# Router logits in four column groups, token rows dealt out anew, and a branch turned round, in a two-layer mixture-of-experts step

## The reference, cut to what matters

```
def moe_swiglu(h, w_router, w_gu, w_down):
    t = h.reshape(B * L, D)
    logits = (t @ w_router).astype(jnp.float32)
    top_v, top_i = lax.top_k(logits, TOP_K)
    top_w = jax.nn.softmax(top_v, axis=-1)
    gates = jnp.einsum('nk,nke->ne', top_w, one_hot(top_i, N_EXPERTS))
    gu = jnp.einsum('nd,edf->enf', t, w_gu)
    g, u = jnp.split(gu, 2, axis=-1)
    eo = jnp.einsum('enf,efd->end', jax.nn.silu(g) * u, w_down)
    y = jnp.einsum('ne,end->nd', gates, eo)

h = rms_norm(x, g_ffn) * (1 + scale2) + shift2
x = x + gate2 * moe_swiglu(h, ...)
```

## Time and profile before

| what | value |
|---|---|
| median of 3 runs | 1887.8 us (1887.16 to 1888.7) |
| the profiled execution | 1886.11 us |
| its span, from the first to the last instruction | 1884.3 us |
| PE busy | 97% of the span |
| DVE / ACT / POOL busy | 59% / 42% / 7% |
| moved by DMA | 290.56 MB, a mean of 154 GB/s |

### The profile page before, as it was taken

One profiled execution on the slowest core, in us unless ns is written; L12 is line 12 of the kernel. 1 busy time (PEld: TensorE's weight loads), 2 busy tenths in 40 slices (PEclk: granted clock), 3 DMA queues, 4 the chain that ended last, 5 costly groups with the idle time before them and its releaser, 6 DMA issues.

```text
span 1884.3 us, 30889 instructions
## 1 busy us (share of the span) xinstructions
PE 1818.4 (97%) x12347; PEld 1680.9 (89%) x12347; DVE 1115.4 (59%) x1907; ACT 789.5 (42%) x1335; POOL 141.1 (7%) x109
## 2 busy tenths in 40 slices
PE   7999989999999999999999889799999999999988
PEld 6999857999999999999999569698989989899886
DVE  2643786544432343456536874476778778778777
ACT  4222264422211222233221554165656656666565
POOL 2000000200000000020000001222000000002221
PEclk8999999999999999999999999899999999999999
DMA  9435100422423224233254001196787778778862
GB/s 363 161 116 217 64 1 1 135 101 101 146 79 112 101 101 146 79 113 123 79 191 145 12 1 23 75 234 215 255 255 248 266 226 277 263 238 292 314 221 79
DMA packets 93847, 290.56 MB, mean 154 GB/s; under 512 B 15368, under 2 KB 23944, under 8 KB 93696
## 3 DMA queue, kind: packets, MB, share of 16 engines
q1 hardware_dynamic: 86784, 271.20, 43.2%
q0 software_dynamic: 6912, 17.30, 2.7%
HBM read 281.98 MB, written 12.28 MB: 156 GB/s over the span
## 4 chain that ended last, share of the span: by engine, by line
PE 87%; DVE 6%; issue 2%; DMA 2%; ACT 2%; POOL 1%; SPq 0%; POOLq 0%; ACTq 0%; DVEq 0%
PE ps L776 48%; PE ps L1144 11%; PE ps L1167 5%; PE ps L1145 5%; PE ps L1177 4%; PE ps L842 3%; PE ps L971 2%; PE ps L917 2%; PE ps L1155 2%; PE ps L1148 2%; DVE nbias L2099 1%; PE ps L1147 1%; DVE pr L2116 1%; DVE w_lo L1943 1%; DMA yab<-y_rows,late 1%
## 5 line engine op out<-in xcount | busy, mean ns | idle before, releaser
L1943 DVE TENSOR_TENSOR w_lo<-raw,w_hi 128x1024 fp32r<-128x1024 f32 x394 | 482.3, 1225 | 345.8 <-ACT w_hi L1383 337.8
L1383 ACT ACTIVATE w_hi<-raw 128x1024 fp32r<-128x1024 f32 x394 | 414.5, 1054 | 315.7 <-PE ps L776 170.8
L1144 PE MATMUL ps<-hg,w_hi 128*128 128x320 f32 (+5 forms) x1232 | 346.8, 351 | 5.0 <-DVE w_lo L1943 3.7
L776 PE MATMUL ps<-a_hi,w_hi 128*128 128x320 f32 x1472 | 341.4, 313 | 3.4 <-DVE a_lo L1974 3.4
L776 PE MATMUL ps<-a_hi,w_lo 128*128 128x320 f32 x1472 | 336.5, 310 | 0.0
L776 PE MATMUL ps<-a_lo,w_hi 128*128 128x320 f32 x1472 | 333.5, 307 | 0.0
L1145 PE MATMUL ps<-hg,w_lo 128*128 128x160 f32 (+5 forms) x1232 | 301.0, 244 | 0.0
L776 PEld LDWEIGHTS ps<-a_hi,w_hi 128*128 128x128 f32 x1472 | 247.0, 188 | 12.1 <-issue 8.1
L776 PEld LDWEIGHTS ps<-a_lo,w_hi 128*128 128x128 f32 x1472 | 248.5, 188 | 0.0
L776 PEld LDWEIGHTS ps<-a_hi,w_lo 128*128 128x128 f32 x1472 | 245.0, 188 | 0.0
L1144 PEld LDWEIGHTS ps<-hg,w_hi 128*128 128x128 f32 x1232 | 232.9, 189 | 6.6 <-DVE w_lo L1943 4.2
(11 more groups left out here) (321 smaller groups left out, 2599.3 us busy)
## 6 DMA issues: line engine op xcount, KB each, us to landing
raw<-gu_w SPq DMA_DIRECT2D x220, 512.0 KB, 4.7
raw<-moe_down_w SPq DMA_DIRECT2D x88, 512.0 KB, 4.4
ada_raw<-ada_w SPq DMA_DIRECT2D x21, 2048.0 KB, 8.2
raw<-in_w SPq DMA_DIRECT2D x48, 512.0 KB, 9.7
raw<-down_w SPq DMA_DIRECT2D x22, 512.0 KB, 3.4
raw<-out_w SPq DMA_DIRECT2D x16, 512.0 KB, 3.6
ada_pro<-ada_w SPq DMA_DIRECT2D x2, 2048.0 KB, 18.8
y_rows<-ey POOLq DMA_DIRECT2D x7, 512.0 KB
```

Source lines behind the costliest of these rows:

```text
L776: ins = nc.tensor.matmul(out[:, hf, 0:c1 - c0], w, o[:, c0:c1], start=f, stop=e)
L1144: nc.tensor.matmul(sums, whi, both, start=(k == 0), stop=False)
L1383: nc.scalar.activation(w_hi[:, s, :], raw[:, n % RAW, :], ACT.Copy).then_inc(hi_done, 1)
L1943: nc.vector.tensor_tensor(w_lo[:, s, :], raw[:, n % RAW, :], w_hi[:, s, :].bitcast(F32), ALU.subtract)\
```

## The change

It has four parts.

1. Logits in column groups. Four feature blocks are multiplied at once, each in its own 32 columns of PE's array, so that four partial sums lie on partitions 0, 32, 64 and 96 onward. They are added when `lgT` is turned: the transposes become products with a small matrix `four_sum`.
2. Rows dealt out anew. DVE does tiles 0, 3 and 4, ACT and POOL only 1 and 2. POOL's second row waits for `mask_ready`. DVE does tile 3 ahead of the one-hot work and tile 4 while PE counts. SP writes the rows in the order 0, 1, 3, 4, 2.
3. The stream is turned (the five `xt`) ahead of PE's branch. The second weight chunk is split behind the gathered rows.
4. On each engine the test is `< 1` in place of `> 0`, and the experts' part stands directly behind it, the general part after it.

```
-ROWS_BY_POOL = 3
+ROWS_BY_POOL = (1, 2)
+ROWS_BY_DVE = (0, 3, 4)
+COL = 32
+GROUPS = P // COL
...
-                    for t in range(TT):
-                        if t < ROWS_BY_POOL:
-                            sp.wait_ge(ht_pool, t + 1)
+                    for t in (0, 1, 3, 4, 2):
+                        if t in ROWS_BY_POOL:
+                            sp.wait_ge(ht_pool, ROWS_BY_POOL.index(t) + 1)
                         else:
-                            sp.wait_ge(ht_dve, t - ROWS_BY_POOL + 1)
+                            sp.wait_ge(ht_dve, ROWS_BY_DVE.index(t) + 1)
...
-                    with sp.If(sp.value_load(most_i[0:1, 0:1], min_val=0, max_val=EXPERTS) > 0):
+                    with sp.If(sp.value_load(most_i[0:1, 0:1], min_val=0, max_val=EXPERTS) < 1):
+                        sp.wait_ge(order_ready, 1)
+                        for e in range(EXPERTS):
...
+                    def logits_of(k0):
+                        last = k0 + GROUPS == KB
+                        pe.wait_ge(h_done, k0 + GROUPS)
+                        for hf in range(2):
+                            for j in range(GROUPS):
+                                nc.tensor.matmul(ps[COL * j:COL * j + EXPERTS, rg % 4, hf, 0:HALF], wr[:, k0 + j, :],
+                                                 hraw[:, k0 + j, hf * HALF:(hf + 1) * HALF],
+                                                 start=(k0 == 0), stop=last and hf == 0)
+                        for j in range(GROUPS):
+                            ins = nc.tensor.matmul(ps[COL * j:COL * j + EXPERTS, rg % 4, 1, HALF:HALF + 2], wr[:, k0 + j, :],
+                                                   mods[:, l, 3 * KB + k0 + j, :], start=False, stop=last)
                         return ins
...
                     for t in range(TT):
-                        nc.tensor.transpose(ps[:, (rg + 2) % 4, 0, t * EXPERTS:(t + 1) * EXPERTS],
-                                            lgT[:, t * P:(t + 1) * P], idn[0:EXPERTS, 0:EXPERTS])
+                        nc.tensor.matmul(ps[:, (rg + 2) % 4, 0, t * EXPERTS:(t + 1) * EXPERTS],
+                                         lgT[:, t * P:(t + 1) * P], four_sum[:], start=True, stop=True)
...
                     tile_rows(5, 3)
-                    fill(rg + 6, FILL["mask"])
+                    tile_rows(6, 4)
+                    fill(rg + 7, FILL["mask"])
                     pe.wait_ge(mask_ready, 1)
...
-                    tile_rows(7, 4)
...
-                    main_expert(MAIN[:1])
+                    main_expert(MAIN[:len(START)])
                     pe.wait_ge(most_ready, 1)
-                    with pe.If(pe.value_load(most_i[0:1, 0:1], min_val=0, max_val=EXPERTS) > 0):
...
+                    with pe.If(pe.value_load(most_i[0:1, 0:1], min_val=0, max_val=EXPERTS) < 1):
+                        main_expert(MAIN[len(START):])
...
-                    for b, t in ((1, 0), (3, 1), (4, 2)):
+                    for b, t in ((3, 1), (4, 2)):
...
                                 gathered(slot, i, gathered_rows(e), ROOM[e])
+                                if (e, i) == (0, 1):
+                                    split_hi(n0 + 1, q0)
...
-                                if i in (2, 4) and part is MAIN:
-                                    split_hi(n0 + i // 2 - 1, q0)
+                                if i == TT - 1 and part is MAIN:
+                                    split_hi(n0, q0)
...
-            for t in range(ROWS_BY_POOL):
-                pool.wait_ge(ht_scaled, t + 1)
+            for i, t in enumerate(ROWS_BY_POOL):
+                pool.wait_ge(ht_scaled, i + 1)
+                if i:
+                    pool.wait_ge(mask_ready, 1)
                 nc.gpsimd.tensor_tensor(ht[:, t, :], ht[:, t, :], shift_rows[:, min(t, 1), :], ALU.add)\
                     .then_inc(ht_pool, 1)
...
+            nc.vector.tensor_reduce(four_sum[:], idn[:].rearrange("p (j r) -> p r j", r=32)[:, 0:EXPERTS, :], AX, ALU.add)\
+                .then_inc(four_ready, 1)
...
-                    token_rows(0)
+                    shifted_rows(1, 0)
                     dve.wait_ge(mm_done, rq + 3)
...
+                    scaled_rows(1)
+                    scaled_rows(2)
+                    shifted_rows(5, 3)
                     link(nc.vector.tensor_copy(tf[:], ti[:]))
...
                     link(nc.vector.memset(before[:, 0, :], 0.0))
-                    token_rows(1)
-                    token_rows(2)
-                    shifted_rows(5, 3)
-                    dve.wait_ge(mm_done, rq + 7)
+                    shifted_rows(6, 4)
+                    dve.wait_ge(mm_done, rq + 8)
...
                     select_ranks()
-                    shifted_rows(7, 4)
                     overflow()
...
```

More of the change, by code:

```diff
@@ L742, in _ @@
                         store_tokens()
[L743 to L754, removed]
             sp.wait_ge(out_done, 16 * 2 * TT)
@@ L1372, in _ @@
                         turn_tokens(lg + TT, POOLED, 1)
+                    with pe.Else():
+                        pe.wait_ge(hst_lo, TT)
+                        with pe.Fori(0, ROUNDS) as r:
+                            experts(EXPERTS // 2 * r)
+                        pe.wait_ge(alo_done, operand[l, "act"] + GENERAL * EXPERT_OPERANDS)
+                        for t in range(TT):
+                            g = mg + GENERAL * EXPERT_BLOCKS + t
+                            open_block(g)
+                            for hf in range(2):
+                                ins = scatter(g, t, hf, 1)
+                            ins.then_inc(mm_done, 1)
+                        turn_tokens(mg + GENERAL * EXPERT_BLOCKS + TT)
         @block.scalar
@@ L1796, in _ @@
                         token_roots()
-                    with act.Else():
-                        main_expert(MAIN)
-                        token_roots(SEEDED, POOLED)
-                        for t in SHARED:
-                            act.wait_ge(mm_done, q0 + MAIN_Q + 2 * TT + t + 1)
-                            for kb in range(4, KB):
-                                ins = nc.scalar.activation(x[:, kb, t * P:(t + 1) * P],
-                                                           ps[:, (g0 + MAIN_G + TT + t) % 4, 1, (kb - 4) * P:(kb - 3) * P],
-                                                           ACT.Copy, scale=gfin[:, kb:kb + 1])
-                            ins.then_inc(yblk_act, 1)
                 if l == 0:
@@ L2742, in _ @@
                     links = chain[0]
-                    with dve.If(dve.value_load(most_i[0:1, 0:1], min_val=0, max_val=EXPERTS) > 0):
+                    with dve.If(dve.value_load(most_i[0:1, 0:1], min_val=0, max_val=EXPERTS) < 1):
+                        main_expert(MAIN_REST)
+                        for t in range(2, TT):
+                            if t < TT - 1:
+                                token_reciprocal(t - 2)
+                            if t == TT - 2:
+                                dve.wait_ge(rows_scaled, 1)
+                                dve.sem_inc(blk_free, 1)
+                            add_tokens(t, g0 + MAIN_G + t, q0 + MAIN_Q + LAST_ORDER.index((t, 1)) + 1)
+                            if t == TT - 2:
+                                token_reciprocal(2)
+                                dve.wait_ge(rows_scaled, 2)
+                                dve.sem_inc(blk_free, TT - 2)
+                        dve.sem_inc(blk_free, 1)
+                        for t in range(TT):
+                            if t < 2:
+                                token_reciprocal(TT - 2 + t)
+                            final_tokens(t, g0 + MAIN_G + TT + t, q0 + MAIN_Q + 2 * TT + t + 1, t in SHARED)
+                    with dve.Else():
+                        chain[0] = links
                         main_expert(MAIN[1:len(START)])
```

108 lines of the change are left out of this document (44 added, 64 removed).

## The result

| kernel | median (range, runs) | before beside it | ratio, 95% interval |
|---|---|---|---|
| changed kernel | 1871.92 us (1868.69 to 1874.09, 4) | 1887.93 us (4 runs) | 0.9919 [0.9905, 0.9933] |

The change makes the kernel 16.0 us faster by these medians, where 12.1 was forecast. Two more sets of the same kernel (experiments 9 and 13) gave ratios of 0.9932 and 0.9916. The mean of the three ratios is 0.9922, a gain of 14.7 us on 1887; by that mean the time would stand at 1873.1, just inside the range.

What follows compares the result with a forecast made beforehand. The experts' part was taken as bound by PE from its first product. Logits 5.5, rows 3.4, SP's jump 1.6, behind the load 1.9, the end -0.3 sum to 12.1 us: 1887.8 to 1875.7, range 1872.8 to 1881.0.

Steps and rivals of the forecast that it cites:

- the one behind the load: From the first weight load to the first product: load unchanged at 7.83 us, 1.9 won behind it, bounds 0.3 and 3.0.
- the end: Program's end: engines jump over the general part, SP's jump hidden in its wait for stores; 0.3 us lost, bounds 0 and 2.5.
- the experts' part: From the first product on: bound by PE, so an earlier first product brings the end forward; own gain 0.
- Logits: Routing stretch: column groups save 6.0 us, dearer turning costs 1.0, DVE's wait gives 0.5; 5.5 in sum.
- DVE's wait of 0.5: At DVE's first logits instruction: the wait for ACT's row 0 goes because DVE does that row itself, 0.5 us.
- Rival D: At the logits: the column groups run in turn, so the 6.0 us falls away; 1881.7 us, 4%.
- Rows: DVE's cast and subtraction in the routing stretch are no longer held by POOL's rows; 3.4 us, bounds 1.0 and 3.4.
- rival C: In the routing stretch POOL's second row holds DVE for a row, 2.4 us less gain; 1878.1 us, 9%.
- SP's jump: At the branch: SP reads the order of the experts without first jumping over the general part, 1.6 us.
- Rival B: Code behind the branch must still be fetched: SP's 1.6 us stays, about 1.5 of ACT's copies follow the weights; 1878.8, 10%.
- Rival E: At the program's end the jump isn't hidden, costing 2.5 us in place of 0.3; 1877.9 us, 5%.
- the turned stream in a shadow: Ahead of the first product: PE's 3.37 us and ACT's delay fall away in the shadow of the weight transfer.

Runs made afterwards that it cites:

- Experiment 1: The kernel before with only the logits in column groups; 1879.43 us, ratio 0.9958.
- experiment 2: The kernel before with only the rows dealt out anew; 1887.13 us, ratio 0.999.
- 3: The kernel before with only the stream turned ahead of the branch and the second chunk split behind the gathered rows; 1891.09 us, ratio 1.0023.
- 8: The changed kernel without the exchanged arms of the branch; 1883.80 us, ratio 0.9983.
- 4 to 7: Kernel before with only branch arms exchanged, 1883.94 us; changed kernel without column groups, 1877.49, without new rows, 1876.15, without early turning, 1874.11.
- Experiment 12: The changed kernel with SP's stores of the result behind the branch instead of in its two parts; 1871.96 us, ratio 0.9915.
- experiment 10: The changed kernel with the general part first again on PE alone, so PE jumps over it; 1879.10 us, ratio 0.996.
- experiment 14: The kernel before with the stream turned ahead of the branch and the arms of the branch exchanged; 1883.98 us, ratio 0.9986.
- Experiment 5: The changed kernel without the logits' column groups, keeping the tile `four_sum` and the instruction that fills it; 1877.49 us, ratio 0.9958.
- experiment 11: The changed kernel with the general part first again on ACT and DVE, so these two jump over it; 1880.86 us, ratio 0.9964.

## Why the prediction was right in direction and short in size

The steps of the sum came to 12.5 for 12.1, and that is partly luck: their errors are +0.9, -0.2, 0, +0.9 and -1.2. Two of them failed as steps, the one behind the load and the end. What took the time below the range is a term that the sum put at nothing, the experts' part.

**Logits.** The mechanism held. The products gave more than the 6.0 taken (PE's first logits to its first transpose 10.42 us before, 3.66 after, 6.8 less), and turning them cost less (1.69 in place of 0.92, +0.8, not +1.0). DVE's wait of 0.5 went, but not because DVE does row 0. Experiment 1, in which ACT still does it, has the same 6.7 us from the last residual to the logits as the changed kernel (13.2 before), and experiment 2, in which DVE does it, has 13.3. The longer turning covers ACT's row too. Together 6.4 for 5.5. Rival D is out.

**Rows.** Right: 3.2 up to the order of the experts, 3.5 up to the overflow test, for 3.4. POOL's second row holds nothing: the five additions of the counts beside it, which have one input in PSUM, took 0.95 us, as before. The first small instruction behind them starts 0.13 us after POOL's row has ended (1202.54 and 1202.67), so none that reads SBUF alone stood beside it. So rival C is out. The Trainium skill ("SBUF — State Buffer", "Who interferes with whom") says that an instruction of VectorE with two inputs in SBUF is held by a GpSimd instruction that reads SBUF, and one with at most one such input isn't, outside certain modes that casts can enter; by that rule, the trace agrees (0.18 and 0.17 for cast and subtraction beside nothing, 1.36 and 2.25 beside POOL's rows in experiment 1).

**SP's jump.** Right, 1.6. Rival B is out: ACT's first instruction behind its branch followed in 0.1.

**Behind the load: a step that failed.** It was put as "The load itself: 7.83 us, shared with the gather, issued as close to it as before, so the same", and 1.9 was won behind it. In the changed kernel the first load lands 5.1 us behind its issue (6.2 and 4.8 in the other two profiles), before ACT has done its fifth copy, and binds nothing. The path runs over the gathered rows. So the whole stage is to be counted from the issue to the first product: 15.1 before and 11.7, 13.1 and 12.1 in the three profiles, 2.8 on the mean for 1.9. What differs among the three is when the gathered rows' transposes start and how long they take, 2.07, 3.00 and 2.42 us; the second profile has:

```profile
1220.02 3.00 PE L1265 MATMUL ps<-idn,gx 128*128 128x128 f32 x16 [3.94 <-DMA gx<-h_rows,slot_row]
```

Why the load lands earlier is not shown. In the five kernels in which every engine jumps (before, 1, 2, 3 and 8), nine or ten packets of instructions come between the overflow test and the first product, and the load took 5.7 to 7.8 us; in the three profiles of the changed kernel and in 4 to 7, in which all fall through, one to three, and 3.4 to 6.2. The two ranges overlap, and with one packet each the changed kernel's own load took 4.8 to 6.2. The loads are also nearer to or farther from the gather (0.1 to 2.7 us), which no run held fixed.

**The end: the other.** 1.5 in place of 0.3. It was put as "its jump (2.5) fits in that", the 3.2 us of SP's wait. SP's jump behind its last store lasts 3.7 to 4.0 us in the three profiles, and the store itself landed 1.0 to 1.2 later. In the first profile the store was the last to arrive: SP's jump ended 0.2 us behind its last packet (1866.23 against 1866.03), and SP went on as soon behind that packet as before, 0.36. In the other two SP's jump came last, by 0.3 and 0.2. Experiment 12 took SP's jump away and the store stayed late. With the late store go PE's fetches, the 16 KB packets on q8. Without a jump at the end (before, 1, 2, 3 and 8) its packets end 2.4 to 2.8 us behind its issue, and in every kernel in which PE jumps there 3.1 to 3.6. In experiment 10 only PE doesn't jump at the end, and they end after 2.7; there SP's jump ends the kernel, 5.9 us behind DVE's last instruction, between 5.1 and 6.6. That is one kernel, in which the other engines' fetches come at other moments too, so the cause is likely and not proven. Rival E had the size (2.5) nearer than the forecast, and its mechanism is part of it.

**Where the parts were weighed.** The sum took parts 3 and 4 as independent, 1.6 for the branch and the turned stream in a shadow. Together they gave 2.6 (experiment 14), near the forecast's 3.2 for these steps (1.6 + 1.9 - 0.3). But part 3 alone loses 4.3. Its trace puts that down to PE's jump, which moves from beside the other engines' jumps to behind them: the gathered rows' transposes start 2.9 us after the rows have landed, where it was 1.4 before, and run at half the clock. The Trainium skill ("Runtime: NRT & Kernel Launch", "Instruction fetch mechanics") says that a taken branch outside what is loaded stalls until its target has been fetched; by that rule, the trace agrees, with 4.96 us for PE. It also says that crossing from one fetched block to the next is mostly hidden; here PE stalled again a few instructions behind a jump, by 3.74 and 1.26, each time until 1.3 to 1.4 us after the next 16 KB packet had ended, so that doesn't hold directly behind a jump.

**What is left: a term put at nothing.** The steps come to 12.5 by three profiles, the times to 14.7, which by the intervals of the ratios are hardly apart. Most of the rest stands in the experts' part, of which the forecast said that "what brings that product forward brings the end forward". It was 1.9 shorter on the mean of three.

One piece of 1.0 us goes with the kernel and not with chance. From the second expert's first product to the seventh's, counted from 1, it took 376.5 us before and 375.5 in all three profiles after; the fourth, which the expectations call the third, has the most of it (75.67 and 75.0). In all eighteen profiles the kernels without the tile `four_sum` take 376.1 to 376.5 and those with it 375.4 to 375.8. Experiment 5, which has the tile but not the groups, takes 375.4. So neither the groups nor the earlier first product makes it, but something that comes with the tile. In the fourth expert it is gained bit by bit over PE's products, with no wait between them. Why is open.

The other piece is chance. In eighteen profiles of all these kernels the experts' part takes 638.3 to 642.2 us and the last residual comes at 1185.5 to 1191.4, over the same code. One source is PE's clock in the seventh expert. PE stands idle there for 2.3 to 2.6 us in each of the three profiles below, and from about the end of that gap the granted clock is at half (1.2 GHz) for 3.4 us in the first profile of the changed kernel, for 6.8 in its third, and not at all in experiment 1. That expert takes 76.7, 78.3 and 75.1 us. Windows of 20 us around the place, in this order:

```profile
1700.00:1720.00 20.00, 17.69 (x125) 17.47 (x125) 16.49 (x42) 11.19 (x25) 9.25 (x7) 0.91 0.73 243
```

```profile
1700.00:1720.00 20.00, 17.38 (x113) 17.15 (x112) 15.69 (x43) 10.36 (x22) 9.50 (x7) 0.83 0.77 260
```

```profile
1713.00:1733.00 20.00, 17.68 (x137) 17.46 (x136) 17.83 (x47) 12.15 (x25) 9.27 (x7) 1.00 0.75 246
```

The profile of before has the second longest experts' part of all, so a part of the miss is the profile that the forecast was made against.

## What to carry to other kernels

A jump over code that isn't loaded costs an engine 2.5 to 6 us here and can stall it again a block later. Jumps that run beside each other and under a transfer cost little, 3.6 us for all of them in the kernel before, and much one behind another, 11.4 in the changed kernel without part 4. So before moving work across a branch, ask in which order the engines come to their jumps, and put the part that runs directly behind the test. The jump then comes at that part's end, which cost 1.5 here. A step that shortens what lies behind a load has to be counted again from the load's issue: once the load isn't the last to arrive, its landing is no longer a term. And a forecast within a few us should know how far profiles of one kernel lie apart: the three of the changed kernel differ by 2.9 us in the experts' part and by 3.0 ahead of the routing stretch.

## What the runs showed of the hardware

The second stall behind a jump (3.74 us, with the next 16 KB packet of instructions at 1224.7) was not expected, nor that ScalarE's jump takes from 4.3 to 6.2 us before its next instruction (4.31 before, 6.17 in experiment 11). Four column groups of 8-column weights gave 0.079 us for an instruction of 320 columns, where one group alone took 0.276. The last store of the kernel took 1.0 to 1.2 us longer to land while four engines fetched code, and only 0.2 longer where PE did not (experiment 10). With the same idle gap of 2.3 us ahead of it, PE's clock fell to half for 3.4 us in one profile and not at all in another.
